# The seam of a gated delta layer: corner blocks stored in two parts, four groups of the gate's projection moved ahead, the first corner blocks taken in other steps

## What is computed

```python
ia = a_mat + jnp.eye(c)                       # (b, h, n, 64, 64), unit lower triangular
u = lax.linalg.triangular_solve(ia, vb, left_side=True, lower=True, unit_diagonal=True)
w = lax.linalg.triangular_solve(ia, kb * jnp.exp(g)[..., None], ...)
def step(s, xs):
    q_c, k_c, u_c, w_c, qk_c, sd_c = xs
    v_new = u_c - w_c @ s
    o_c = q_c @ s + qk_c @ v_new
    return s * sd_c[..., None, None] + k_c.T @ v_new, o_c
...
gate = jax.nn.silu(z.reshape(bsz, t, GDN_V_HEADS, GDN_HEAD_V))
o = rms_norm(o, norm_w) * gate
return o.reshape(bsz, t, GDN_V) @ w_out
```

## Time and profile before

| | |
|---|---|
| median of three runs | 3055.72 us (3054.97 to 3056.46) |
| the profiled execution | 3056.0 us, of which its span is 3054.2 us |
| mean granted TensorE clock | 0.97 |
| TensorE, VectorE, ScalarE, GpSimd busy | 93%, 60%, 39%, 22% |
| the layer's front | about 1960 to 2234 us of the span |
| the layer's back | 2234 to about 2460 us |

### The profile page before, as it was taken

How to read it: one execution, slowest core, us unless ns; L and a number is a source line. 1 busy time by engine, 2 the same in 40 slices (tenths; PEclk the granted TensorE clock), 3 DMA queues, 4 the chain that set the end, 5 groups by cost and what they waited for, 6 DMA issues and landing times. The chain is left out here.

```text
span 3054.2 us, 39241 instructions
## 1 busy us (share of the span) xinstructions
PE 2830.6 (93%) x14634; PEld 2440.5 (80%) x14634; DVE 1838.0 (60%) x3337; ACT 1204.6 (39%) x2120; POOL 668.6 (22%) x402
## 2 busy tenths in 40 slices
PE   7989879989989999999999999799969979999998
PEld 6879548779889998998888888688757757788877
DVE  4434543359997888676887887645924544344442
ACT  3433542232326766432333333367424433222221
POOL 0013110004332333365332332043022310000000
PEclk9999999999999999999999999899989989999999
DMA  3202112333437888999999999467365531322232
GB/s 125 83 24 77 50 42 87 134 135 128 140 114 242 293 313 297 349 386 375 367 359 353 361 360 354 170 197 211 128 196 151 145 119 61 110 96 96 96 103 69
DMA packets 251468, 572.34 MB, mean 187 GB/s; under 512 B 43616, under 2 KB 152032, under 8 KB 222272
## 3 DMA queue, kind: packets, MB, share of 16 engines
q1 hardware_dynamic: 212160, 426.56, 41.7%
q0 software_dynamic: 36864, 134.23, 11.2%
q10 hardware_dynamic: 2304, 9.70, 0.9%
HBM read 486.38 MB, written 84.02 MB: 187 GB/s over the span
## 5 line engine op out<-in xcount | busy, mean ns | idle before, releaser
L43 PE MATMUL pe_ps<-hh,pe_uh 128*128 128x384 f32 x1024 | 350.1, 342 | 16.9 <-issue 14.4
L45 PE MATMUL pe_ps<-hh,pe_ul 128*128 128x384 f32 x1024 | 344.7, 337 | 0.0
L44 PE MATMUL pe_ps<-hl,pe_uh 128*128 128x384 f32 x1024 | 344.5, 336 | 0.0
L43 PE MATMUL pe_ps<-pe_vh,pe_whi 128*128 128x512 f32 x768 | 299.7, 390 | 3.0 <-DVE pe_vl L1682 3.0
L45 PE MATMUL pe_ps<-pe_vh,pe_wlo 128*128 128x512 f32 x768 | 299.3, 390 | 0.0
L44 PE MATMUL pe_ps<-pe_vl,pe_whi 128*128 128x512 f32 x768 | 299.3, 390 | 0.0
L1511 POOL DMA_INDIRECT pe_gu<-in_u_rows,pe_urow x128 | 200.6, 1568 | 304.7 <-DVE pe_gu L1643 280.9
L1519 POOL DMA_INDIRECT pe_gv<-in_v_w,pe_vrow x128 | 159.1, 1243 | 328.2 <-DVE pe_acc L1652 315.1
L43 PEld LDWEIGHTS pe_ps<-hh,pe_uh 128*128 128x128 f32 x1024 | 194.2, 190 | 18.8 <-issue 18.5
L1643 DVE SCALAR_TENSOR_TENSOR pe_gu<-pe_gu,pe_xs 128x1024 f32<-128x1024 f32 x128 | 155.4, 1222 | 85.5 <-DMA pe_gu<-in_u_rows,pe_urow 85.3
L44 PEld LDWEIGHTS pe_ps<-hl,pe_uh 128*128 128x128 f32 x1024 | 194.1, 190 | 0.3
(11 more groups left out here) (591 smaller groups left out, 6990.3 us busy)
## 6 DMA issues: line engine op xcount, KB each, us to landing
xu<-in_u_w SPq DMA_DIRECT2D x64, 1024.0 KB, 6.3
pe_v_raw<-in_v_w SPq DMA_DIRECT2D x64, 1024.0 KB, 8.4
hidden_scratch<-pe_hs SPq DMA_DIRECT2D x64, 384.0 KB, 8.6
gate_scratch<-pe_stage SPq DMA_DIRECT2D x24, 1024.0 KB, 11.0
pe_hw<-hidden_scratch SPq DMA_DIRECT2D x64, 384.0 KB, 4.8
pe_gate<-gate_scratch SPq DMA_DIRECT2D x64, 384.0 KB, 5.4
gf_raw<-in_gdn_w SPq DMA_DIRECT2D x16, 1024.0 KB, 6.8
gb_pk<-pk_scratch SPq DMA_DIRECT2D x64, 256.0 KB, 2.8
```

What stands on the lines that cost most here:

```text
L43: pe.matmul(out, lh, rh, start=start, stop=False)
L44: pe.matmul(out, lh, rl, start=False, stop=False)
L45: return pe.matmul(out, ll, rh, start=False, stop=stop)
```

## The change

- **Front, stores.** SyncE stores only key heads 0 and 1 of both halves (`store_blocks` with heads 0 to 2, four transfers of 16 rows x 16 KB), `rc` first, in iteration 14, and loads the first blocks after `rc_out` and then `u_out`. These stand ahead of, or among, the `vb` stores of heads 5 to 7. The stores of `vb` of heads 6 and 7 signal `first.kept` in place of the front's own semaphores, and the front doesn't wait for them.
- **Front, z.** The first z tile is loaded in iteration 13, right after its place is free. GpSimd clears the back's tiles and casts the z tile ahead of its wait for the elimination. TensorE does four of the eight k of z tile 0 ahead of the transposes of the last head; both phases share one tensor of PSUM.
- **Back, stores.** GpSimd stores key heads 2 to 7 of both (four transfers of 48 rows x 16 KB, signal `rest_out`) from its own queue, between its memsets and its first split. SyncE waits for `rest_out` in step 1. `area` and `vb` therefore keep their place below the end of `ot`; ScalarE waits for both signals ahead of the first write to `ot`.
- **Back, order.** For c = 0 blocks 2, 3, 4, 5 are due in steps 1, 2, 4, 5 in place of 0, 1, 2, 5. In step 0 no z group is issued.

```diff
+def store_blocks(sp, dram, tile, a, heads, signal):
+    rows = slice((a * GDN_KH + heads.start) * NCH, (a * GDN_KH + heads.stop) * NCH)
+    sp.dma_start(dram[a, heads].rearrange("h i c t -> (h i) (c t)"), tile[rows, :]).then_inc(signal, 16)
...
                 def keep_v(m):
                     sp.wait_ge(vb_ok, m + 1)
-                    sp.dma_start(packed(m, GDN_VB), vb[m % 2][:]).then_inc(vb_out[m % 2], 16)
+                    sp.dma_start(packed(m, GDN_VB), vb[m % 2][:]).then_inc(vb_out[m % 2] if m < KH - 2 else first.kept, 16)
+                def load_first(dram, tiles, signals):
+                    for l in range(2):
+                        for a in range(2):
+                            half = slice(a * C, (a + 1) * C)
+                            sp.dma_start(tiles[l][half, :, half], dram[a, l, 0:4].rearrange("i c t -> c i t")).then_inc(signals[l], 16)
...
+                    if it == KH + 5:
+                        low_done(sp, NB - 2)
+                        sp.dma_start(first_z.raw[:], first_z.src).then_inc(first_z.raw_in, 16)
+                    if it == KH + 6:
+                        sp.wait_ge(elim, 2 * (H - 1))
+                        sp.wait_ge(turned_u, 1)
+                        sp.wait_ge(kept_u, 1)
+                        sp.wait_ge(cleared, 1)
+                        for a in range(2):
+                            store_blocks(sp, rc_dram, flat(at), a, slice(0, 2), rc_out)
+                        for a in range(2):
+                            store_blocks(sp, ud_dram, utf, a, slice(0, 2), u_out)
                     if it > KH:
                         keep_v(it - KH - 1)
                     if it == KH + 6:
-                        sp.wait_ge(elim, 2 * (H - 1))
-                        sp.dma_start(ud_dram.rearrange("a h i c t -> (a h i) (c t)"), utf).then_inc(u_out, 16)
-                        sp.wait_ge(turned_u, 1)
-                        sp.wait_ge(kept_u, 1)
-                        sp.wait_ge(cleared, 1)
-                        sp.dma_start(rc_dram.rearrange("a h i c t -> (a h i) (c t)"), flat(at)).then_inc(u_out, 16)
-                low_done(sp, NB - 2)
-                sp.dma_start(first_z.raw[:], first_z.src).then_inc(first_z.raw_in, 16)
-                sp.wait_ge(u_out, 32)
-                sp.wait_ge(first.zeroed, 4)
...
+                        sp.wait_ge(first.zeroed, 4)
+                        sp.wait_ge(rc_out, 32)
+                        load_first(rc_dram, first.rc, first.rc_in)
+                        sp.wait_ge(u_out, 32)
+                        load_first(ud_dram, first.ub, first.ub_in)
                 keep_v(KH - 1)
                 for b in range(2):
-                    sp.wait_ge(vb_out[b], 16 * (KH // 2))
+                    sp.wait_ge(vb_out[b], 16 * (KH // 2 - 1))
...
-                pool.wait_ge(elim, 2 * (H - 1))
-                pool.memset(at[:, H:C, H:C], 0.0).then_inc(cleared, 1)
                 pool.wait_ge(proj, NB - 1)
...
                 pool.tensor_copy(first_z.wh[:], first_z.raw[:]).then_inc(first_z.w_hi, 1)
+                pool.wait_ge(elim, 2 * (H - 1))
+                pool.memset(at[:, H:C, H:C], 0.0).then_inc(cleared, 1)
...
+                        if m == KH - 1:
+                            pe.wait_ge(first_z.w_hi, 1)
+                            pe.wait_ge(first_z.w_lo, 1)
+                            pe.wait_ge(vb_ok, KH - 1)
+                            for k in range(GDN_Z0):
+                                mm3(pe, ps[:, GDN_BZ, :], (first_z.wh[:, k, :], first_z.wl[:, k, :]), (hh[:, k, :], hl[:, k, :]), k == 0, False)
                         pe.wait_ge(silu_ok, 4 * KH + m + 1)
...
-            n = {0: 4 * c + 2, 1: 4 * c + 3, 2: 4 * c + 4, 5: 4 * c + 5}.get(i, NM)
+            n = {(0 if c else 1): 4 * c + 2, (1 if c else 2): 4 * c + 3, (2 if c else 4): 4 * c + 4, 5: 4 * c + 5}.get(i, NM)
...
                 load_z(2)
+                sp.wait_ge(first.kept, 32)
...
+                    if g == 1:
+                        sp.wait_ge(first.rest_out, 16 * 4)
...
                 pool.memset(m1[:], 0.0).then_inc(zeroed, 1)
+                for a in range(2):
+                    store_blocks(pool, rc_dram, first.at, a, slice(2, KH), first.rest_out)
+                    store_blocks(pool, ud_dram, first.ut, a, slice(2, KH), first.rest_out)
                 split(1)
...
-                        for k in range(KD):
+                        for k in range(GDN_Z0 if f == 0 else 0, KD):
...
-                    next(ahead, None)
+                    if g:
+                        next(ahead, None)
```

More of the change, by code:

```diff
@@ L133, in __init__ @@
         self.ub = [nc.alloc_sbuf_tensor_at(f"gb_ub0{l}", shape, F32, offset=TOP - (16 - 2 * l) * 1024) for l in range(2)]
-        self.zeroed = nc.alloc_semaphore("gb_first_zeroed")
+        self.zeroed, self.kept, self.rest_out = (nc.alloc_semaphore(f"gb_first_{n}") for n in ("zeroed", "kept", "rest_out"))
         self.rc_in, self.ub_in = ([nc.alloc_semaphore(f"gb_first_{n}{l}") for l in range(2)] for n in ("rc_in", "ub_in"))
@@ L1824, in _, with gdn_front @@
                     last.then_inc(back, 1)
-GDN_F = 640
+GDN_F, GDN_BZ, GDN_Z0 = 640, 5, 4
 GDN_QK, GDN_KD, GDN_VB, GDN_AT = (slice(a, b) for a, b in ((0, 256), (256, 384), (384, 512), (512, 640)))
-def gdn_front(nc, hh, hl, ident, gcols, rows_dram, sd_dram, ad_dram, ud_dram, rc_dram, pk_dram, drams, first, first_z):
+def store_blocks(sp, dram, tile, a, heads, signal):
+    rows = slice((a * GDN_KH + heads.start) * NCH, (a * GDN_KH + heads.stop) * NCH)
+    sp.dma_start(dram[a, heads].rearrange("h i c t -> (h i) (c t)"), tile[rows, :]).then_inc(signal, 16)
+def gdn_front(nc, ps, hh, hl, ident, gcols, rows_dram, sd_dram, ad_dram, ud_dram, rc_dram, pk_dram, drams, first, first_z, ot_end):
     w_dram, ba_dram, conv_dram, alog_dram, dt_dram, reset_dram, mask_dram = drams
@@ L1839, in gdn_front @@
         raw = [nc.alloc_sbuf_tensor_at(f"gf_raw{u}", weights, F32, offset=at0[u] + 16 * 1024) for u in range(2)]
+        area = ph.sb("area", [P, 2 * C * C + 1536])
+        vb = [ph.sb(f"vb{u}", [P, NCH, P]) for u in range(2)]
+        assert nc.sbuf_base <= ot_end
         bah, bal = (ph.sb(n, [P, KD, P], F32R) for n in ("bah", "bal"))
@@ L1850, in gdn_front @@
         kd = [ph.sb(f"kd{u}", [P, NCH, P]) for u in range(2)]
-        vb = [ph.sb(f"vb{u}", [P, NCH, P]) for u in range(2)]
         junk = ph.sb("junk", [P, NCH, P])
-        area = ph.sb("area", [P, 2 * C * C + 1536])
         small = ph.sb("small", [P, 4])
@@ L1889, in gdn_front @@
          silu_ok, sq_ok, ss_mm, ssq_ok, kk_ok, ktr_ok, dif, dd_ok, e_ok, ke_ok, qe_ok, kd_ok, ssk_ok, vtr_ok, vb_ok, zeroed,
-         ones_ok, at_in, bt_in, rt_in, rho_v, rho_a, rho_mm, rr_ok, scaled, elim, u_out, row_v2, conv_in, w_lo0, w_lov, turned_u, kept_u, cleared) = (
+         ones_ok, at_in, bt_in, rt_in, rho_v, rho_a, rho_mm, rr_ok, scaled, elim, u_out, rc_out, row_v2, conv_in, w_lo0, w_lov, turned_u, kept_u, cleared) = (
             ph.sem(n) for n in ("small_in ba_in ba_hi ba_lo logits row_v row_a rows_out r_in turned cols_ok w_hi w_lo proj tap0 "
@@ L1893, in gdn_front @@
                                 "vb_ok zeroed ones_ok at_in bt_in rt_in rho_v rho_a rho_mm rr_ok scaled elim "
-                                "u_out row_v2 conv_in w_lo0 w_lov turned_u kept_u cleared").split())
+                                "u_out rc_out row_v2 conv_in w_lo0 w_lov turned_u kept_u cleared").split())
         w_in, g_in, kqp_out, ke_out, qe_out, kd_out, vb_out = (
@@ L1921, in share @@
             return mine
+        first.at, first.ut = flat(at), utf
         with nc.Block() as block:
@@ L2349, in _, with gdn_back @@
                         last.then_inc(vtr_ok, 1)
-def gdn_back(nc, hh, hl, ot, ident, gcols, sd_dram, ud_dram, rc_dram, pk_dram, drams, first, first_z, nxt):
+def gdn_back(nc, ps, hh, hl, ot, ident, gcols, sd_dram, ud_dram, rc_dram, pk_dram, drams, first, first_z, nxt):
     w_dram, gain_dram = drams
@@ L2389, in gdn_back @@
         full = [P, NCH, P]
-        BO, BZ, BT = 4, 5, 7
+        BO, BZ, BT = 4, GDN_BZ, 7
         NM = 4 * STEPS
@@ L2605, in _ @@
                     if c and i in (5, 7):
+                        if c == 1 and i == 5:
+                            act.wait_ge(first.rest_out, 16 * 4)
+                            act.wait_ge(first.kept, 32)
                         finish(i // 7, c - 1)
@@ L2973, in second_block @@
         gcols = sb("gcols", [P, 4, GDN_KH, NCH], F32, o)
[L2974 to L2977, removed]
+        with nc.psum_tensor("gdn_ps", [P, 8, 512], F32) as ps:
+            gdn_front(nc, ps, hh, hl, ident, gcols, rows_dram, sd_dram, ad_dram, ud_dram, rc_dram, pk_dram,
+                      [a[n] for n in ("gdn_w", "gdn_ba", "gdn_conv", "a_log", "dt_bias", "reset", "gdn_mask")], gb_first, z_first,
+                  nc.sbuf_base + 4 * KD * T * 4)
+            ot = (sb("oth", [P, 2 * KD, T], F32R, o), sb("otl", [P, 2 * KD, T], F32R, o))
```

(1 more changed line is left out.)

7 lines of the change are left out of this document (removed).

## The result

The changed kernel takes 3062.42 us in the median of 11 runs (3060.88 to 3067.58), the kernel before 3056.46 us in 11 runs beside it. The ratio is 1.0019, with a 95% interval of 1.0011 to 1.0027: 6 us slower, where 5.3 us faster was forecast. The time lies above the range. (The prediction started from the 3055.72 us of an earlier set of three runs.)

The account below looks back on a forecast made before the run. TensorE is 93% busy, so only its gaps at the seam, chiefly 13.13 us from SyncE's store queue, can be won: 7.6 - 0.5 + 3.3 + 1.4 - 6.5 = 5.3 us off, median 3050.4 us, range 3043.5 to 3059.

Parts of the forecast that it names:

- part 1: Front's end: small urgent stores first and the last `vb` landing not awaited start the back earlier; gain 7.6 us (5.9 to 9.1).
- the cast: Front: GpSimd's z cast, moved under VectorE's elimination, delays it by 0 to 1.04 us; 0.5 taken.
- Part 2: Back's start: later corner blocks and z groups done in the front save 3.3 us, block 4's move 1.4 us.
- step 0 in the wait: Back: step 0's two solves and one spread run while TensorE waits for block 2's `gb_rc`; 0.5 us.
- the wait at step 3: Back: TensorE's wait for VectorE's `gb_r` at g = 3 goes as block 4 moves later; gain 1.4 us, bounds 0 and 1.4.
- the early z: Four z groups done in the front ahead of the last transposes spare the back 2.8 us.
- Part 3: Back's start: 3 MB of late stores go ahead of the first loads and delay `gb_rc`; 6.5 us paid, bounds 0 and 13.8.
- (b): Rival, back's stores: 48 partitions hold the DMA engines twice as long, 13.8 us paid; 3057.7 us, chance 0.10.
- (a): Rival, back's start: stores and loads overlap, 0 to 4.5 us paid; 3043.9 to 3048.4 us, chance 0.34.
- (c): Rival, back's stores: three times as long through GpSimd's slow issue and the loads' packets, 20.7 us paid; 3064.6 us, chance 0.08.
- (d): Rival, front: 16-row stores take over 12 us to land, most of the 7.6 us gain goes; 3058 us, chance 0.06.
- The rule against this part: Back's stores: partitions 0 to 63 reach only half the DMA ports; some 16 us for the stores, the gain gone.

## Why the prediction was wrong

- **What bounds the kernel, part 1.** Right. The chain of SP's queue was the 13.13 us: B came 6.75 us earlier, 7.1 forecast. Its terms: 2.8 us for the landing, confirmed by putting the wait back in one execution; the z groups delay the last transposes as worked out (issued from 2221.36, through in 4.3 us; 4.4 forecast) with a clock at half; the cast delays the elimination by 0.7 us (0.5 taken). SP wasn't the last: the stores of 16 rows landed in 4.6 and 6.0 us, not 4.2, the `vb` of head 6 was issued at 2225.30, and SP then waited 3.0 us for the `vb` of head 7, where about 5 us to spare were forecast.
- **Part 2.** Right in the sum: 4.54 us, 4.7 forecast. Its terms, read one by one from the runs on the kernel with whole stores, were less exact: 1.7 us for step 0 in the wait (0.5 taken), 1.26 for the wait at step 3 (1.4), 2.3 behind block 2 for the early z (2.8). That the sum fits better than its terms is partly luck.
- **Part 3, the term that failed.** The mechanism was named right in the main (the stores get ahead of the loads, and `gb_rc` is later for it), the size was not: 6.5 us taken, 14.9 paid. The stores don't come wholly first either: 14.9 us are paid of the 20.5 that they take alone. The failing step is the rate: 3.1 MB at 500 GB/s, or at that of 4.2 MB in 12 us, gave the 6.3 to 8.9 us. Both rates are of tiles with all 128 partitions; the stores have 48 of one half, at 150 GB/s. The sum with 14.9 in place of 6.5 is 3.1 us slower than before, and the stretch shows 4.25.
- **Rivals.** (b), half rate, was this mechanism, with 13.8 us and a chance of 0.10; its time, 3057.7, is still 4.7 us short, of which 0.7 is the other median of the kernel before. The timed difference, 6.0 us, has an interval of 3.4 to 8.3, in which the stretch's 4.25 lies; the sum's 3.1 is just below it. (a) falls: the stores do not overlap with the loads at no cost. (c) named a slow issue on GpSimd's queue; it took 2.1 us for all four. (d) falls: it needed over 12 us for the landing of the 16-row stores, which took 4.6 and 6.0.
- **The rule against this part**, that of the Trainium skill on the ports, was quoted, its result called a loss of the gain, and its nearest rival (b) then given a tenth. With its estimate of some 16 us for the price, the sum would have been 4.2 us slower; the stretch shows 4.25. That it fits so closely is partly luck, as the stores alone take 20.5 us. "The trace of before has no store from part of the partitions" was true, and it should have widened the forecast: a price taken from rows of another shape needs a word on which part of the shape matters.
- **The range.** Its upper end, 3059, took in (b) but not (c); the blind spot was to give (c) another cause (GpSimd's slow issue, which proved fast) in place of a larger price for the same one.

What stays open: the stores alone take 20.5 us, block 2 starts at B + 14.65 without them and at B + 29.59 with them, so some 5 us overlap. How an engine shares its time between the two queues was not measured, nor was the load on a single port of the on-chip memory.

## What to carry to other kernels

A transfer that takes some rows of a tile isn't cheaper in proportion: look where its partitions lie, and take its rate from a row with the same partitions, or measure it alone. Before splitting a store so that an urgent part may go first, try the whole store in the right order, with the readers' loads right behind the half they need. And when a step is moved to another queue and time, its new neighbours decide: here the four stores of 48 rows cost 14.9 us ahead of the first loads and 8.2 us behind them (a stretch of 284.51 against 276.33), and whole tiles 8.3 us ahead of them and nothing that the stretch shows behind them (275.58).

## What the runs showed of the hardware

Stores of 16 KB rows to HBM ran at 148 to 153 GB/s from 48 partitions of one half of the partitions and at 281 GB/s from 48 partitions across the middle (40 to 87), and rows of 12 KB at 338 GB/s from all 128 (the last two with start and landing in the time). The queue made no difference: 12.3 and 12.4 us to landing from SyncE and GpSimd. A plain store on GpSimd's queue took 0.5 us to issue. Beside a GpSimd cast, one VectorE subtraction with both inputs in on-chip memory took 1.28 us in place of 0.56. In the 1.8 us from block 2's start TensorE was granted the full clock (1.00) after a gap of 1.51 us, and a mean of 0.60 after one of 3.38 us.
